# A conformer trunk in fp32r pairs: weights refilled ahead of the norm's row, another order of the opening, and pairwise sums in the last norm

## What is computed

```python
for l in range(DEPTH):
    h = swiglu_ffn(rms_norm(x, ffn1_norm_pre[l]), ffn1_w_in[l], ffn1_w_out[l])
    x = x + 0.5 * rms_norm(h, ffn1_norm_post[l])
    h = rms_norm(x, mix_norm_pre[l]) @ mix_w_in[l]
    o_gdn = gated_deltanet_group(h, conv_w, a_log, dt_bias, out_g)   # 4 heads of 128, blocks of tokens
    o_cm = conformer_conv_group(h, dw_w, dw_b, ln_g, ln_b)           # 512 channels, 31 taps
    h = jnp.concatenate([o_gdn, o_cm], axis=-1) @ mix_w_out[l]
    x = x + rms_norm(h, mix_norm_post[l])
    h = swiglu_ffn(rms_norm(x, ffn2_norm_pre[l]), ffn2_w_in[l], ffn2_w_out[l])
    x = x + 0.5 * rms_norm(h, ffn2_norm_post[l])
    x = rms_norm(x, block_norm[l])
```

## Time and profile before

| | |
|---|---|
| median of three runs | 2261.32 us |
| the profiled execution | 2260.7 us |
| its span in the trace | 2259.0 us |
| mean granted clock of TensorE | 0.959 |
| PE busy | 2114.6 us, 94% |
| DVE busy | 1241.4 us, 55% |
| ACT busy | 682.3 us, 30% |
| read from HBM | 174.38 MB |

### The profile page before, as it was taken

How to read it: one execution, slowest core, us unless ns; L and a number is a source line. 1 busy time by engine, 2 the same in 40 slices (tenths; PEclk the granted TensorE clock), 3 DMA queues, 4 the chain that set the end, 5 groups by cost and what they waited for, 6 DMA issues and landing times.

```text
span 2259.0 us, 26304 instructions
## 1 busy us (share of the span) xinstructions
PE 2114.6 (94%) x10076; PEld 1769.3 (78%) x10076; DVE 1241.4 (55%) x1708; ACT 682.3 (30%) x910; POOL 39.5 (2%) x51
## 2 busy tenths in 40 slices
PE   6999999897888899999989999999979799999998
PEld 5788888776887688888778888877759777888887
DVE  4555522699766554542275554357997655555322
ACT  3222222424324422222242222233342343222222
POOL 0000000000110000000000000000010000000000
PEclk9999999999899899999989999999979999999997
DMA  4333333233001133333323333323320023333320
GB/s 127 112 93 93 90 101 100 64 82 87 10 1 47 47 110 98 99 87 101 92 67 102 93 93 93 101 66 85 84 65 1 1 66 89 98 93 91 101 78 38
DMA packets 345792, 177.54 MB, mean 79 GB/s; under 512 B 8338, under 2 KB 344692, under 8 KB 345716
## 3 DMA queue, kind: packets, MB, share of 16 engines
q1 hardware_dynamic: 344058, 176.34, 27.3%
q10 hardware_dynamic: 1658, 0.16, 0.1%
HBM read 174.38 MB, written 2.10 MB: 78 GB/s over the span
## 4 chain that ended last, share of the span: by engine, by line
PE 78%; DVE 16%; ACT 3%; issue 2%; SPq 1%; DMA 0%; DVEq 0%; ACTq 0%
PE res L447 23%; PE res L448 23%; PE res L449 23%; DVE u L1211 6%; DVE cacc L1292 2%; DVE wl L1066 1%; PE stat L454 1%; PE pq L654 1%; PE pq L447 1%; PE pq L448 1%; PE pq L449 1%; ACT wh L776 1%; PE bc L475 1%; DVE pre L1278 1%; PE res L673 1%
## 5 line engine op out<-in xcount | busy, mean ns | idle before, releaser
L447 PE MATMUL res<-xh,wh 128*128 128x512 f32 x1696 | 666.6, 393 | 27.4 <-DVE xl L1080 27.4
L448 PE MATMUL res<-xl,wh 128*128 128x512 f32 x1696 | 664.6, 392 | 0.0
L449 PE MATMUL res<-xh,wl 128*128 128x512 f32 x1696 | 664.0, 392 | 0.0
L776 ACT ACTIVATE wh<-raw 128x1024 fp32r<-128x1024 f32 (+1 forms) x336 | 347.9, 1037 | 1038.6 <-PE res L449 1004.0
L1066 DVE TENSOR_TENSOR wl<-raw,wh 128x1024 fp32r<-128x1024 f32 (+1 forms) x336 | 402.4, 1198 | 399.6 <-ACT wh L776 398.8
L447 PEld LDWEIGHTS res<-xh,wh 128*128 128x128 f32 x1696 | 321.5, 190 | 96.1 <-DVE xl L1080 28.8
L449 PEld LDWEIGHTS res<-xh,wl 128*128 128x128 f32 x1696 | 321.3, 189 | 67.6
L448 PEld LDWEIGHTS res<-xl,wh 128*128 128x128 f32 x1696 | 321.7, 190 | 66.7
L447 PE MATMUL res<-hh,wh 128*128 128x512 f32 x704 | 273.9, 389 | 0.0
L448 PE MATMUL res<-hl,wh 128*128 128x512 f32 x704 | 273.9, 389 | 0.0
L449 PE MATMUL res<-hh,wl 128*128 128x512 f32 x704 | 273.9, 389 | 0.0
(11 more groups left out here) (255 smaller groups left out, 1758.1 us busy)
## 6 DMA issues: line engine op xcount, KB each, us to landing
raw<-in_ffn_w_in SPq DMA_DIRECT2D x176, 512.0 KB, 3.8
raw<-in_ffn_w_out SPq DMA_DIRECT2D x64, 448.0 KB, 3.7
raw<-in_mix_w_in SPq DMA_DIRECT2D x48, 512.0 KB, 4.0
raw<-in_ffn_w_out SPq DMA_DIRECT2D x32, 512.0 KB, 3.8
raw<-in_mix_w_out SPq DMA_DIRECT2D x16, 512.0 KB, 3.9
xin<-in_x SPq DMA_DIRECT2D x4, 512.0 KB, 5.0
out_dram<-xin SPq DMA_DIRECT2D x4, 512.0 KB, 4.0
crows<-in_cm_dw_w ACTq DMA_DIRECT2D x1, 62.0 KB
```

Source lines behind the costliest of these rows:

```text
L447: pe.matmul(bank, wh[:, slot, j, :], hi, start=first, stop=False)
L448: pe.matmul(bank, wh[:, slot, j, :], lo, start=False, stop=False)
L449: return pe.matmul(bank, wl[:, slot, j, :], hi, start=False, stop=last)
L776: act.activation(wh[:, slot, 0:nk, :], raw[:, slot, 0:nk, :], ACT.Copy).then_inc(hi_full, 1)
```

## The change

It has five parts. Units 5 and 6 of a stage get their high half right behind `root` on ACT and their low half right behind `row` on DVE, and unit 4 gets its high half before the seventh square and its low half before the last sum. In `first_units` PE does, for each tile, the six matmuls that need only the high half of x, then the three that need the low half; `x_sums` moves into unit 3, ahead of its sixth tile, and the spread ahead of the second tile of unit 4 (not in layer 1's first FFN). The opening issues four units of weights before layer 1's constants, lets DVE copy even tiles and ACT odd ones, turns layer 0's constants in the middle of x and layer 1's behind unit 5, splits weights between the tiles of x, and runs units 0, 1, 2 one after another. The exponential and the sign of the decay constants move into each layer's mixer. The last norm adds squares in pairs on DVE and has four sums on PE in place of eight. The diff is cut to its core and moved to the left.

```diff
             w_out = ffn_w[f][1].rearrange("l (k p) c -> l p k c", p=P)
-            with sp.Fori(0, KF // 2) as i:
+            def two_pairs(i):
                 for q in range(2):
...
                              w_in[l, :, :, bass.ds(col, P)], l)
+            first = f == 0 and l == 0
+            if first:
+                two_pairs(0)
+                for later in range(1, L):
+                    load_constants(sp, later, s_rows2, s_heads2)
+            with sp.Fori(int(first), KF // 2) as i:
+                two_pairs(i)
             with sp.Fori(0, KD // 4) as i:
...
     pe.wait_ge(s_load, 16 * NC)
+    def turn_constants(l, bank):
+        pe.wait_ge(s_rows if l == 0 else s_rows2, 16 * 13 * max(l, 1))
+        for which, n in ((0, ROWS_A), (1, ROWS_B)):
+            pe.transpose(bank[:, which * P:which * P + n], crows[0:n, l, which, :],
+                         ident[0:n, 0:n]).then_inc(s_cturn, 1)
     for k in range(KD):
+        if k == 4:
+            turn_constants(0, pq[:, 0, :])
         if k >= 4:
-            pe.wait_ge(x_turned, k - 3)
+            pe.wait_ge(x_turned_b if k % 2 else x_turned, (k - 4) // 2 + 1)
         for c in range(NC):
...
         mm.then_inc(s_xturn, 1)
-    pe.wait_ge(s_rows, 16 * 13)
-    pe.wait_ge(s_rows2, 16 * 13 * (L - 1))
-    for l in range(L):
-        for which, n in ((0, ROWS_A), (1, ROWS_B)):
-            pe.transpose(pq[:, 0, (2 * l + which) * P:(2 * l + which) * P + n], crows[0:n, l, which, :],
-                         ident[0:n, 0:n]).then_inc(s_cturn, 1)
     def tile(bank, slot, j, hi, lo, first, last):
...
     def first_units(u0, stage, stat_q, l):
-        for k in range(KD):
-            pe.wait_ge(xs_ready, l * NXS + stage * KD + k + 1)
+        banks = [in_bank(unit_bank(n, stage, l)) for n in range(4)]
+        if stage == 0 and l == 0:
+            for n in range(3):
+                pe.wait_ge(lo_full, u0 + n + 1 + SLOTS)
+                for k in range(KD):
+                    if n == 0:
+                        pe.wait_ge(xs_ready, k + 1)
+                    mm = tile(banks[n], n, k, xh[:, k, :], xl[:, k, :], k == 0, k == KD - 1)
+                mm.then_inc(unit_done, 1)
+        for k in range(KD if stage or l else 0):
+            pe.wait_ge(xh_ready, l * NXS + stage * KD + k + 1)
             for n in range(3):
...
                     pe.wait_ge(lo_full, l * UNITS + (u0 + n + 1 + SLOTS))
-                mm = tile(in_bank(unit_bank(n, stage, l)), n, k, xh[:, k, :], xl[:, k, :], k == 0, k == KD - 1)
+                pe.matmul(banks[n], wh[:, n, k, :], xh[:, k, :], start=k == 0, stop=False)
+                pe.matmul(banks[n], wl[:, n, k, :], xh[:, k, :], start=False, stop=False)
+            pe.wait_ge(xs_ready, l * NXS + stage * KD + k + 1)
+            for n in range(3):
+                mm = pe.matmul(banks[n], wh[:, n, k, :], xl[:, k, :], start=False, stop=k == KD - 1)
                 if k == KD - 1:
...
         pe.wait_ge(y_done, YB + (3 * l + stage) * KD)
-        in_unit(u0 + 3, 3, unit_bank(3, stage, l), l)
-        x_sums(stage, l)
+        pe.wait_ge(lo_full, l * UNITS + (u0 + 3 + 1 + SLOTS))
+        two = stage == 0 and l > 0
+        for k in range(KD):
+            if k == KD - 3 and not two:
+                x_sums(stage, l)
+            mm = tile(banks[3], 3, k, xh[:, k, :], xl[:, k, :], k == 0, k == KD - 1)
+        mm.then_inc(unit_done, 1)
+        if two:
+            x_sums(stage, l)
         pe.wait_ge(lo_full, l * UNITS + (u0 + 4 + 1 + SLOTS))
         for k in range(KD):
-            if k == KD - 2:
+            if k == (KD - 2 if two else 1):
                 spread(stat_q, l)
...
         in_unit(u0 + 5, 1, 5, l)
-        if stage == 0 and l > 0:
+        if two:
             spread_block(l)
+        if stage == 0 and l == 0:
+            pe.wait_ge(rs_ready, 1)
+            for later in range(1, L):
+                turn_constants(later, bc[:, (later - 1) * 2 * P:])
...
         ffn(1, l)
+    def pair_sums(p):
+        pe.wait_ge(xpair, p + 1)
+        token_sums((sqr, sqb)[p % 2][:, 0, :], first=p == 0, last=p == KD // 2 - 1).then_inc(ssq_full, 1)
     for k in range(KD):
...
         act.activation(rsq[:], stat[:, 0:NC], ACT.Sqrt, bias=eps[:, 0:1], scale=1.0 / D).then_inc(root_ready, 1)
-    def inputs(stage, gain, l):
+    def inputs(stage, gain, u0, l):
         for k in range(KD):
             if stage == 0 and l == 0:
-                act.wait_ge(x_turned, k + 1)
+                if k == 0:
+                    act.wait_ge(s_cc, 1)
+                if k == 4:
+                    high(1, 1, 8, l)
+                act.wait_ge(x_turned_b if k % 2 else x_turned, k // 2 + 1)
             else:
...
             act.activation(xh[:, k, :], xt[:, k, :], ACT.Copy, scale=gain[:, k:k + 1]).then_inc(xh_ready, 1)
+        if stage == 0 and l == 0:
+            high(2, 2, 8, l)
+            high(3, 3, 8, l)
         two = stage == 0 and l > 0
         for k in range(KD):
+            if k == KD - 2:
+                high(u0 + SLOTS, 0, 8, l)
             if k > 2:
...
         if f == 0:
-            inputs(0, gpre[:, l, :], l)
+            if l == 1:
+                act.wait_ge(s_one, L - 1)
+            inputs(0, pre_gain(l), u0, l)
         else:
-            inputs(2, call[:, l, G_F2PRE:G_F2PRE + KD], l)
-        high(u0 + SLOTS, 0, 8, l)
+            inputs(2, call[:, l, G_F2PRE:G_F2PRE + KD], u0, l)
         root([0, 4][f], l)
+        for n in range(1, 3):
+            high(u0 + n + SLOTS, n, 8, l)
         if f == 0 and l > 0:
...
         row_out([0, 4][f], 2 * f, l)
-        def pair(p, odd, sizes=(8, 8), first=0):
-            for half in range(first, 2):
+        def pair(p, odd, sizes=(8, 8), ahead=0):
+            for half in range(ahead, 2):
                 high(p * 2 + (u0 + 4 + half), 2 * odd + half, sizes[half], l)
...
             act.activation(gs[:, odd, :], gs[:, odd, :], ACT.Silu).then_inc(silu_done, 1)
-        pair(0, 0, first=1)
-        pair(1, 1)
+        pair(0, 0, ahead=2)
+        pair(1, 1, ahead=1)
         pair(2, 0)
...
     act.wait_ge(s_mask, 3)
-    act.wait_ge(s_heads, 16 * 3)
-    act.wait_ge(s_heads2, 16 * 3 * (L - 1))
-    for l in range(L):
-        act.activation(hcall[:, l, 0, :], hcall[:, l, 0, :], ACT.Exp).then_inc(s_negA, 1)
-    for n in range(SLOTS):
-        high(n, n, 8, 0)
-    act.wait_ge(s_one, L)
+    def odd_tile(k):
+        act.wait_ge(s_xturn, k + 1)
+        act.activation(xt[:, k, :], res[:, k % 4, :], ACT.Copy).then_inc(x_turned_b, 1)
+    odd_tile(1)
+    odd_tile(3)
+    high(0, 0, 8, 0)
+    odd_tile(5)
+    odd_tile(7)
     for l in range(L):
         ffn(0, l)
-        inputs(1, call[:, l, G_MPRE:G_MPRE + KD], l)
-        high(MBASE + SLOTS, 0, 8, l)
+        inputs(1, call[:, l, G_MPRE:G_MPRE + KD], MBASE, l)
         root(2, l)
+        for r in range(1, 3):
+            high(MBASE + r + SLOTS, r, 8, l)
         row_out(2, 1, l)
         for r in range(MIX_IN_U):
-            if r > 0:
+            if r > 2:
                 high(MBASE + r + SLOTS, r % SLOTS, 8, l)
...
             if r == 2 * CT + 3 * H:
+                act.wait_ge(s_heads if l == 0 else s_heads2, 16 * 3 * max(l, 1))
+                act.activation(hcall[:, l, 0, :], hcall[:, l, 0, :], ACT.Exp).then_inc(s_negA, 1)
                 act.wait_ge(na_ready, l + 1)
...
         ffn(1, l)
+    def last_square(k):
+        if k >= 4:
+            act.wait_ge(ssq_full, 6 * L + k // 2 - 1)
+        act.activation((sqr, sqb)[k // 2 % 2][:, k % 2, :], xt[:, k, :], ACT.Square).then_inc(xsq_ready, 1)
     for k in range(KD):
         act.wait_ge(x_ready, L * NXR - KD + k + 1)
+        if k == KD - 1:
+            last_square(k)
         act.activation(yg[:, k, :], xt[:, k, :], ACT.Copy,
                        scale=call[:, L - 1, G_BLOCK + k:G_BLOCK + k + 1]).then_inc(xg_ready, 1)
-        if k > 2:
-            act.wait_ge(ssq_full, 6 * L + k - 1)
...
+    def constants(l, which, bank):
+        n, at0 = ((ROWS_A, 0), (ROWS_B, ROWS_A))[which]
+        dve.wait_ge(s_cturn, 2 * l + 2)
+        dve.tensor_copy(call[:, l, at0:at0 + n], bank[:, which * P:which * P + n]).then_inc(s_cc, 1)
+    def half_gains(l):
+        dve.wait_ge(s_cc, 4 * l + 2)
         for g in (G_F1POST, G_F2POST):
-            dve.wait_ge(s_cc, 3 * L)
             dve.tensor_scalar(call[:, l, g:g + KD], call[:, l, g:g + KD], 0.5, None,
                               ALU.mult).then_inc(s_cc, 1)
-    dve.wait_ge(s_cc, 5 * L)
-    dve.tensor_copy(gpre[:, 0, :], call[:, 0, G_F1PRE:G_F1PRE + KD]).then_inc(s_one, 1)
-    for l in range(1, L):
-        dve.tensor_tensor(gpre[:, l, :], call[:, l, G_F1PRE:G_F1PRE + KD], call[:, l - 1, G_BLOCK:G_BLOCK + KD],
-                          ALU.mult).then_inc(s_one, 1)
-    dve.wait_ge(s_one, L)
-    dve.wait_ge(x_turned, KD)
+    def later_constants():
+        for l in range(1, L):
+            for which in range(2):
+                constants(l, which, bc[:, (l - 1) * 2 * P:])
```

(52 more changed lines are left out.)

53 lines of the change are left out of this document (26 added, 27 removed).

## The result

The changed kernel takes 2206.26 us, median of four runs (2205.42 to 2211.58); the kernel before took 2264.11 in the same comparison. The ratio is 0.9747, with a 95% interval of [0.9721, 0.9773]: 2.5% faster. The forecast was 2201, with a range of 2192 to 2215. The profiled execution took 2205.52 us.

What follows compares the result with a forecast made beforehand. PE's work plus its holes bound the kernel, except the mixers, set by DVE. Gains of 15.8 + 7.0 + 9.0 + 7.6 + 7.0 + 8.4 + 5.0 = 59.8 us from 2260.7 gave about 2201 us, range 2192 to 2215.

Steps and rivals of the forecast that it cites:

- Refill in the FFNs: Feed-forward stages, unit 5: the 5.30 us wait goes, with 2.36 to 2.96 us of slow steps behind it.
- Refill in the mixer, bound by DVE: Mixers: DVE sets the end, so only its chain counts: two splits (2.26 us) and about 0.8 us on ACT spared.
- the earlier sums and spread: Mixers: sums three tiles earlier and spread at tile 1 of unit 4, 15 matmuls earlier in all, 3.4 us.
- Early start: Five stage starts, not the opening: PE starts on xh alone, 1.24 us earlier, and keeps it.
- the slow steps behind the start stay: Stage starts: the clock has already fallen at the new start, so the low-clock steps remain.
- The sums' new hole: PE ahead of x_sums: a new wait of 0.5 us in four stages, 1.3 in layer 1's first FFN.
- The opening: First stage: first matmul near 17.0 us, unit 3 8.2 us earlier; 15.8 us in all with unit 5's gain.
- The last norm: End of kernel: half of PE's sums go (6.0 us), DVE adds pairs; 5.0 us gained, between 3 and 6.
- the mixers' steps: Both mixers: DVE's chain starts 4.1 us earlier and is spared splits; 7.0 us gained each.
- the one at 2211: Rival: late data starts PE at 22 in the opening, last norm stays PE-bound; 10 us less gain; chance 0.10.
- 2200.9 and 0.6: Whole kernel: forecast profiled execution, and how much higher the median of the runs is; given as 2201.
- the read at 443.42: Mixer: DVE's read of unit 4, ending a stretch from `ga` at 433.86, forecast to take 6.5 us.

Runs made afterwards that it cites:

- Run 1: Kernel before, with the refill of units 5 and 6 ahead of the row in the four feed-forward stages only; 2227.38 us.
- Run 2: Kernel before, with the refill of units 5 and 6 ahead of the row in the two mixers only; 2257.75 us.
- run 3: Kernel before, with only the matmul order of the first three units changed, products with xh first; 2262.43 us.
- run 6: Changed kernel, with unit 4's splits put back behind the squares in layer 1's first feed-forward alone; 2210.70 us.
- run 4: Changed kernel, with four transposes of the last norm's third token block moved behind the wait for the last update; 2203.48 us.
- run 7: Changed kernel, with layer 1's constants issued on SyncE ahead of the first weight units instead of behind them; 2213.75 us.
- run 8: The kernel of run 4, with unit 4's splits put back behind the squares in the five stages after the opening; 2209.18 us.
- run 9: The kernel of run 8, with six small unused matmuls ahead of the first matmul of the five stages after the opening; 2209.06 us.
- runs 5, 10 and 12: Filler matmuls: nine ahead of five starts on the changed kernel, 2215.83 us; 8 and 28 per mixer on run 4, 2205.66 us; and run 12.
- run 12: The kernel of run 9, with 11 and 44 filler matmuls per mixer ahead of the waits for gate_g and Wm; 2208.04 us.
- Run 11: The kernel before, unchanged, measured and profiled once more; 2261.96 us.

## Why the prediction came out right, step by step

- **Refill in the FFNs.** Right, and the largest part. Run 1's four FFNs are 33.0 us shorter for a forecast of 32 (its median 36.5); the wait and the slow steps behind it went and nothing took their place.
- **Refill in the mixer, bound by DVE.** Right. Run 2 shows 2.2 and 2.8 us at `Wm` for 3.1, and run 3 gives 0.9 and 0.5 for the early start. `Wm` came 6.2 and 6.0 earlier in the changed kernel, for 7.0. The other 3 us are what is left for the earlier sums and spread, forecast at 3.4; these were not run alone. What the forecast left out is the scan: +1.3 us in layer 0, -0.7 in layer 1, with the same code.
- **Early start.** The mechanism was right, its size not. The start is 1.2 us earlier, but "the slow steps behind the start stay" was wrong: summed over half-microsecond stretches behind five starts they grew from 22.7 to 26.3 us of low clock. Run 3 keeps 0.4 to 0.9 of 1.24. Behind the norm's sums nothing of it is left in the FFNs. In layer 0's second FFN unit 3 still starts 0.6 us earlier behind the spread than in run 1 (22.0 for 22.6), but unit 5 starts at 35.3 (756.45 - 721.11) for 35.4 (770.57 - 735.21). That the sums for the FFNs still met the forecast is in part luck: run 1 has 10.0 in that stage for 8.2, where the low clock behind the start also happened to be shorter (2.9 us for 5.7 before).
- **The sums' new hole.** 0.34 in four stages for 0.5; in layer 1's first FFN 0.33 for 1.3, and run 6 prices that order at 0.6 us.
- **The opening.** 16.3 for 15.8. The first matmul came at 16.73 for 17.0, at the upper clock; run 4's opening ran at the low one and ended 1.3 us later, for the 1.4 that I gave. Of the 7.5 us by which the first matmul is earlier, run 7 shows 2.6 as the work of SP's order; how the copies on two engines, the earlier splits and units 0, 1, 2 in turn share the rest was argued and not run.
- **The last norm.** This step failed: 5.0 forecast, 0.5 measured. I counted sums and DVE's pairs and missed that the transpose of tile 4 into `bc` waits for the last of eight updates (`x_ready`, `L * NXR`), because DVE still reads the row in `bc`. Before, PE came to it 13.7 us behind the spread and found the update done (the line below has no idle time). With the sums halved PE comes to it after 11.0 us and waits to 14.9, and the pair sum queued behind it holds back ACT's seventh square. Run 4 gets 2.8 us back. The row's spread also ran at the low clock this time (2.07 us for 8 records; 1.16 before). That costs 0.9: in run 8, with run 4's last norm and the spread at the upper clock, the root comes 18.3 us behind the spread for 19.2. The forecast had 17.4 (2245.05 - 2227.68); the last 0.9 no run explains.

PE's turn of tile 4 into `bc` in the kernel before:

```profile
2241.40 0.42 PE L760 MATMUL bc<-ident,yg 128*128 128x128 f32 x1
```

So 59.8 forecast against 55.2: 4.5 of the 4.6 us lie in the last norm, and 1.8 us too many in the mixers' steps stand against 1.1 too few in the opening and the FFNs and 0.6 from the scans. Of the rivals only the one at 2211 named the last norm, and it too had the reason wrong: PE was not bound by its own work there, it waited for DVE's last update, and the opening did its work. Two slips of the forecast change nothing: 2200.9 and 0.6 make 2201.5, and the read at 443.42 is DVE's fifth and not its fourth.

## What to carry to other kernels

When work in front of a wait is halved, list every wait in that engine's queue and put the new arrival time against each: one that cost nothing before can be the next bound, and the instructions queued behind it suffer with it. Price an edit by the stage in which it acts, between two fixed instructions of the same engine: here a total 5.6 us above run 4's hid gains of 9.4 us and losses of 17.9 in run 9. And a low clock only costs where the engine would have worked; in runs 5, 10 and 12 filling holes to keep it up gave nothing in the total, as the data for what follows was not there or the low clock came later.

## What I had not expected of the hardware

- The scan behind `Wm`, the same instructions in all kernels, took between 178.0 and 187.8 us. In the six profiled mixers in which `Wm` came 158.2 to 159.6 us behind the spread it took 183.8 to 187.8, and in nine of the ten at 160.6 to 161.7 it took 178.6 to 178.7 (the tenth 179.8). In the twelve with a later `Wm`, at 162.1 to 167.8, it took 178.0 to 180.0 nine times and 184.5 to 185.0 three times, so an early `Wm` is not the only way to a long scan. The difference goes with the low clock: from `Wm` to the next spread it summed to 22 to 27 us where the scan took 178.0 to 180.0, and to 31 to 41 us where it took 183.8 to 187.8. What sets where it falls is open: a filled head (run 12) did not bring the short scan back, and no run here moved the scan alone.
- PE ran at 0.51 on average for the 21 us of run 9's second stretch while it was busy for 19.8 of them, all with matmuls of 128 x 128 or smaller. A busy PE is no sign of the upper clock.
- The low stretch behind one and the same start differed: layer 0's second FFN had 5.7 us of it behind the start in the kernel before and 2.9 in run 1, with the same code between the spread and the start. The Trainium skill (TensorE: Matmul & The Clock Gate, What's actually happening) says that the count of slow matmuls at a start varies from run to run of one kernel. Run 11 agrees in kind: from 24 to 36 us, behind the opening's start, the granted clock was 0.74 where the first profile of the same kernel has 0.80, and the opening ended 1.1 us later.
